# Turned-form products of a decoder block in fp32: joining two 256-column matmuls into one of 512

## The reference, cut to what matters

```python
def hybrid_layer(x, ...):
    h = rmsnorm(x, g_mix) @ w_in                       # [256, 2048] @ [2048, 5728]
    ...                                                # Mamba-2 scan and sparse attention
    x = x + jnp.concatenate([y_ssd, y_att], axis=-1) @ w_out
    u = rmsnorm(x, g_mlp) @ w_up                       # [2048, 8192]
    return x + jnp.square(jax.nn.relu(u)) @ w_down     # [8192, 2048]

def second_block(x, ...):
    h = fox_attention(rmsnorm_2(x, g0), w_in, b_f, w_out)   # q, k, v: 3 x [2048, 2048], 16 heads
    x = x + rmsnorm_2(h, g1)
    h = sqrelu_mlp(rmsnorm_2(x, g2), w1, w2)                # [2048, 8192], [8192, 2048]
    return x + rmsnorm_2(h, g3)
```

## Time and profile before

| | |
|---|---|
| median of 3 runs | 2294.41 us (2293.33 to 2296.01) |
| profiled execution, own time | 2293.16 us |
| its span | 2291.4 us |
| TensorE busy (matmul) | 2261.6 us, 99% |
| DVE busy | 1208.5 us, 53% |
| ACT busy | 946.4 us, 41% |
| DMA moved | 412.12 MB, mean 180 GB/s |
| granted TensorE clock, mean | 0.998 |

### The profile page before, as it was taken

The page is one execution under the profiler, slowest core; times in us unless marked ns, Lnnn a source line. Parts: engine busy times, 40 slices in busy tenths (PEclk is TensorE's granted clock), DMA queues, the critical chain, the costliest instruction groups (busy, mean ns, idle before and its releaser), DMA issues.

```text
span 2291.4 us, 32313 instructions
## 1 busy us (share of the span) xinstructions
PE 2261.6 (99%) x14211; PEld 2024.1 (88%) x14211; DVE 1208.5 (53%) x1167; ACT 946.4 (41%) x901; POOL 12.4 (1%) x34
## 2 busy tenths in 40 slices
PE   7999999999999999999999999999999999999998
PEld 7988778999988899988899987888998888999886
DVE  5688665545444354544455444555555443545444
ACT  5453564444433343434334434434435333434332
POOL 1000000000000000000000000000000000000000
PEclk9999999999999999999999999999999999999999
DMA  8445435666555666555555454555665556665554
GB/s 259 152 157 166 156 129 190 196 184 183 184 190 193 186 184 183 184 184 184 185 184 183 148 165 155 176 186 171 184 184 192 185 184 188 185 184 189 190 184 147
DMA packets 210908, 412.12 MB, mean 180 GB/s; under 512 B 12804, under 2 KB 12896, under 8 KB 210160
## 3 DMA queue, kind: packets, MB, share of 16 engines
q1 hardware_dynamic: 210368, 409.89, 55.7%
q0 software_dynamic: 432, 0.62, 0.2%
HBM read 408.39 MB, written 2.10 MB: 179 GB/s over the span
## 4 chain that ended last, share of the span: by engine, by line
PE 98%; DVE 1%; ACT 1%; DMA 0%; issue 0%; DVEq 0%; SPq 0%; ACTq 0%
PE bank L1705 16%; PE bank L1706 16%; PE bank L1707 16%; PE bank L1720 15%; PE bank L1723 15%; PE bank L1722 15%; PE bank L1803 1%; PE bank L1735 1%; PE bank L1828 0%; PE bank L1837 0%; PE bank L1922 0%; PE bank L1896 0%; PE bank L1815 0%; PE bank L1807 0%; PE bank L1829 0%; DMA G<-in_g_mix_dram 0%
## 5 line engine op out<-in xcount | busy, mean ns | idle before, releaser
L942 DVE TENSOR_TENSOR wl<-raw,wh 128x2048 fp32r<-128x2048 f32 x380 | 870.3, 2291 | 647.3 <-ACT wh L501 645.2
L501 ACT ACTIVATE wh<-raw 128x2048 fp32r<-128x2048 f32 x380 | 726.7, 1913 | 724.8 <-DMA raw<-in_mlp_w_dram 265.0
L1720 PE MATMUL bank<-XH,wh 128*128 128x256 f32 x2880 | 817.7, 284 | 0.2 <-issue 0.2
L1723 PE MATMUL bank<-XH,wl 128*128 128x256 f32 x2880 | 812.7, 282 | 0.0
L1722 PE MATMUL bank<-XL,wh 128*128 128x256 f32 x2880 | 810.3, 281 | 0.0
L1722 PEld LDWEIGHTS bank<-XL,wh 128*128 128x128 f32 x2880 | 547.2, 190 | 0.6 <-issue 0.5
L1720 PEld LDWEIGHTS bank<-XH,wh 128*128 128x128 f32 x2880 | 543.7, 189 | 3.7 <-issue 2.2
L1723 PEld LDWEIGHTS bank<-XH,wl 128*128 128x128 f32 x2880 | 542.8, 188 | 0.0
L1707 PE MATMUL bank<-wh,hl 128*128 128x512 f32 x1024 | 404.5, 395 | 0.0
L1706 PE MATMUL bank<-wl,hh 128*128 128x512 f32 x1024 | 404.4, 395 | 0.0
L1705 PE MATMUL bank<-wh,hh 128*128 128x512 f32 x1024 | 402.2, 393 | 0.0
(11 more groups left out here) (310 smaller groups left out, 819.7 us busy)
## 6 DMA issues: line engine op xcount, KB each, us to landing
raw<-in_mlp_w_dram SPq DMA_DIRECT2D x128, 1024.0 KB, 5.4
raw<-in_w_up_dram SPq DMA_DIRECT2D x64, 1024.0 KB, 5.5
raw<-in_w_down_dram SPq DMA_DIRECT2D x64, 1024.0 KB, 5.0
raw<-in_fox_w_in_dram SPq DMA_DIRECT2D x48, 1024.0 KB, 5.1
raw<-in_w_in_dram SPq DMA_DIRECT2D x44, 1024.0 KB, 5.0
raw<-in_w_out_dram SPq DMA_DIRECT2D x16, 1024.0 KB, 5.1
raw<-in_fox_w_out_dram SPq DMA_DIRECT2D x16, 1024.0 KB, 5.1
G<-in_norm_g_dram SPq DMA_DIRECT2D x4, 1024.0 KB, 5.9
```

The lines of the kernel that those rows point to most:

```text
L501: act.activation(wh[:, j, :, :], raw[:, j, :, :], ACT.Copy).then_inc(hi_ready, 1)
L942: dve.tensor_tensor(wl[:, j, :, :], raw[:, j, :, :], wh[:, j, :, :].bitcast(F32), ALU.subtract)\
L1720: pe.matmul(o, sh, mh, start=first and kk == 0 and f % 2 == 0, stop=False, skip_group_check=True)
L1723: mm = pe.matmul(o, sl, mh, start=False, stop=last and kk == 3, skip_group_check=True)
```

## The change

`XH` and `XL` become two halves of one tensor `XHL`, laid side by side for each k tile. A new form `half_cols` takes a panel as two half panels of 256 columns. For each k tile and 128-column block it issues one matmul of the high weights with 512 moving columns (high x, then low x) into a whole bank, and one of the low weights with high x into the left half of the same bank. The result of a block is then the sum of the bank's two halves. A half panel uses one pair of banks, so the numbering of accumulators changes (`up_acc`, `fox_acc`). The weights of a half panel come as two chunks of 8 k tiles by 256 columns (`half_panels`), still 1 MB each.

All turned panels of the MLPs and of the fox stage but the first of each use it; `WIN` does not. In the MLPs ACT copies the right half of each bank to `LP` (`part`), DVE adds it to the left half into `RB` and makes Relu and square in one instruction, and `high` and `low` follow on 256 columns. In the fox stage ACT copies the right half straight to `FQ` or `FK`, and DVE adds the left half and multiplies by the factor (`fox_part`), at every second slot, behind the attention work of that slot. The scores wait for a new semaphore, `fqk_ready`. The Fori loops of the MLPs are written out. The diff leaves out the old `relu`, `high`, `square`, `low` and `hidden`, which stand above, and a layout change of the instructions that write `XH` and `XL`.

```diff
-        XH = sb("XH", [P, KT, TOK], F32R)
-        XL = sb("XL", [P, KT, TOK], F32R)
+        XHL = sb("XHL", [P, KT, 2, TOK], F32R)
+        XH, XL = XHL[:, :, 0, :], XHL[:, :, 1, :]
...
+        def up_acc(half, n):
+            return 2 * n - (1 if half == 0 and n else 0)
+        O_DOWN = [up_acc(half, UP) for half in range(2)]
+        O_HALF = O_DOWN[0] + DOWN
+        B_FOX, O_FOX = B_M1 + 2 * B_HALF, O_M1 + O_HALF + O_DOWN[1] + DOWN
+        def fox_acc(n):
+            return O_FOX + (2 * n - (1 if n else 0) if n <= 8 else 7 + n)
...
+            def half_panels(w, b, col):
+                for j in range(4):
+                    sp.wait_ge(chunk_used, 4 * b + j - 3)
+                    c, r = col + 256 * (j // 2), 8 * P * (j % 2)
+                    sp.dma_start(raw[:, j, :, :].rearrange("p a (c n) -> p (a c) n", n=256),
+                                 w[r:r + 8 * P, c:c + 256].rearrange("(k p) n -> p k n", p=P))\
+                      .then_inc(raw_landed[j], 16)
...
-                    with sp.Fori(0, UP // 2 - 1) as i:
-                        for s in (1, 2):
-                            for j in range(4):
-                                chunk(w_a, b + 2 * i + s, j, 4 * j,
-                                      bass.ds(half * HALF + 512 * (2 * i + s), 512))
-                    panel(w_a, b + UP - 1, 0, half * HALF + 512 * (UP - 1))
+                    for n in range(1, UP):
+                        half_panels(w_a, b + n, half * HALF + 512 * n)
...
+                def whole(u, o, b):
+                    act.wait_ge(chunk_used, 4 * b + 4)
+                    for k in range(2):
+                        act.wait_ge(hl_ready, 2 * u + k + 1)
+                        act.activation(RB[:, k, :], acc[o % 2][k][:, :], ACT.Relu).then_inc(acc_freed[o % 2][k], 1)
+                def part(u, o, b, j):
+                    act.wait_ge(chunk_used, 4 * b + j + 1)
+                    for k in range(2):
+                        act.wait_ge(sq_ready, 2 * u)
+                        act.activation(LP[:, k, :], acc[o % 2][k][:, TOK:], ACT.Copy).then_inc(part_ready, 1)
+                def high(u, tile, wide):
+                    for k in range(2):
+                        act.wait_ge(sq_ready, 2 * u + k + 1)
+                        f = 2 if wide else 1
+                        act.activation(hh[:, tile + f * k:tile + f * k + f, :],
+                                       RB[:, k, 0:f * TOK].rearrange("p (f t) -> p f t", f=f), ACT.Copy)\
+                           .then_inc(hh_ready, 1)
+                def hidden(j, half, n, b):
+                    if j >= 2:
+                        if half == 0 and n == 0:
+                            return
+                        u, e, wide, tile = up_acc(half, n), 1, False, 4 * n
+                    else:
+                        n, b = n - 1, b - 1
+                        if n < 0:
+                            return
+                        u, e, wide, tile = up_acc(half, n + 1) - 1, 3, half == 0 and n == 0, 4 * n + 2
+                        if wide:
+                            tile = 4 * n
+                    o, u = o0 + half * O_HALF + u, u0 + half * U_HALF[0] + u
+                    if j % 2:
+                        high(u, tile, wide)
+                    elif wide:
+                        whole(u, o, b)
+                    else:
+                        part(u, o, b, e)
...
+            def fox_part(n, j):
+                acc_o = fox_acc(n) + j // 2
+                act.wait_ge(chunk_used, 4 * (B_FOX + n) + j + 1)
+                kind, f = FOX[n][0], 4 * (n // 2) + j - 1
+                for k in range(2):
+                    dst = FQ if kind == "fq" else FK
+                    act.activation(dst[:, f + k, :], acc[acc_o % 2][k][:, TOK:], ACT.Copy)\
+                       .then_inc(step["fqk_part"], 1)
...
             def fox_side(n):
+                if 1 <= n // 4 <= 8 and n % 4 in (0, 2):
+                    p, e = n // 4 - (n % 4 == 0), 3 if n % 4 == 0 else 1
+                    if 1 <= p <= 7:
+                        fox_part(p, e)
                 if n == 3:
                     root(2, 2)
...
+                def square(u, o, wide):
+                    for k in range(2):
+                        if wide:
+                            dve.wait_ge(acc_freed[o % 2][k], o // 2 + 1)
+                            dve.tensor_tensor(RB[:, k, :], RB[:, k, :], RB[:, k, :], ALU.mult).then_inc(sq_ready, 1)
+                        else:
+                            dve.wait_ge(hl_ready, 2 * u + k + 1)
+                            dve.wait_ge(part_ready, 2 * (u - u // U_HALF[1] - (1 if u % U_HALF[1] else 0)) + k + 1)
+                            dve.tensor_tensor(RB[:, k, 0:TOK], acc[o % 2][k][:, 0:TOK], LP[:, k, :], ALU.add)\
+                               .then_inc(acc_freed[o % 2][k], 1)
+                    if not wide:
+                        for k in range(2):
+                            dve.wait_ge(acc_freed[o % 2][k], o // 2 + 1)
+                            dve.scalar_tensor_tensor(out=RB[:, k, 0:TOK], in0=RB[:, k, 0:TOK], scalar=0.0,
+                                                     in1=RB[:, k, 0:TOK], op0=ALU.max, op1=ALU.mult)\
+                               .then_inc(sq_ready, 1)
+                def low(u, tile, wide):
+                    f = 2 if wide else 1
+                    for k in range(2):
+                        dve.wait_ge(hh_ready, 2 * u + k + 1)
+                        at = slice(tile + f * k, tile + f * k + f)
+                        dve.tensor_tensor(hl[:, at, :], RB[:, k, 0:f * TOK].rearrange("p (f t) -> p f t", f=f),
+                                          hh[:, at, :].bitcast(F32), ALU.subtract).then_inc(hl_ready, 1)
+                def hidden(j, half, n):
+                    if j >= 2:
+                        if half == 0 and n == 0:
+                            return
+                        u, wide, tile = up_acc(half, n), False, 4 * n
+                    else:
+                        n = n - 1
+                        if n < 0:
+                            return
+                        u, wide = up_acc(half, n + 1) - 1, half == 0 and n == 0
+                        tile = 4 * n if wide else 4 * n + 2
+                    o, u = o0 + half * O_HALF + u, u0 + half * U_HALF[0] + u
+                    if j % 2:
+                        low(u, tile, wide)
+                    else:
+                        square(u, o, wide)
...
+            def fox_part(n, j):
+                acc_o = fox_acc(n) + j // 2
+                kind, f = FOX[n][0], 4 * (n // 2) + j - 1
+                dst = FQ if kind == "fq" else FK
+                for k in range(2):
+                    dve.wait_ge(step["fqk_part"], 4 * n - 4 + j - 1 + k + 1)
+                    dve.tensor_tensor(dst[:, f + k, :], acc[acc_o % 2][k][:, 0:TOK], dst[:, f + k, :], ALU.add)\
+                       .then_inc(acc_freed[acc_o % 2][k], 1)
+                for k in range(2):
+                    dve.wait_ge(acc_freed[acc_o % 2][k], acc_o // 2 + 1)
+                dve.scalar_tensor_tensor(out=dst[:, f:f + 2, :], in0=dst[:, f:f + 2, :],
+                                         scalar=SCALE if kind == "fq" else 1.0,
+                                         in1=RCf[:, :].unsqueeze(1).broadcast_to([P, 2, TOK]),
+                                         op0=ALU.mult, op1=ALU.mult).then_inc(step["fqk_ready"], 1)
...
                     attn_probs(1, (n - 18) // 2, Lf, FST)
+                if 1 <= n // 4 <= 8 and n % 4 in (0, 2):
+                    p, e = n // 4 - (n % 4 == 0), 3 if n % 4 == 0 else 1
+                    if 1 <= p <= 7:
+                        fox_part(p, e)
...
-                    if j == 0 and prev:
+                    if j == 0 and prev and not 2 <= n <= 8:
                         take(*prev)
-                prev = (kind, O_FOX + n, seen.get(kind, 0), B_FOX + n)
+                prev = (kind, fox_acc(n), seen.get(kind, 0), B_FOX + n)
...
+            def half_cols(b, o):
+                for j in range(4):
+                    x, e = o + j // 2, j % 2
+                    if e == 0:
+                        acc_wait(x)
+                    pe.wait_ge(lo_ready, 4 * b + j + 1)
+                    for kk in range(8):
+                        k = 8 * e + kk
+                        at = 256 * (kk % 2)
+                        for f in range(2):
+                            bk = acc[x % 2][f]
+                            sh, sl = (z[:, j, kk // 2, at + f * P:at + (f + 1) * P] for z in (wh, wl))
+                            pe.matmul(bk[:, :].rearrange("p (s t) -> p s t", s=2), sh, XHL[:, k, :, :],
+                                      start=k == 0, stop=False, skip_group_check=True)
+                            mm = pe.matmul(bk[:, 0:TOK], sl, XH[:, k, :], start=False, stop=k == KT - 1,
+                                           skip_group_check=True)
+                    mm.then_inc(chunk_used, 1)
+                    yield j
```

(76 more changed lines are left out.)

94 lines of the change are left out of this document (41 added, 53 removed).

## The result

The changed kernel takes 2281.29 us (median of 4 runs, 2279.7 to 2281.62) where the kernel before took 2295.21 us (2293.33 to 2296.66): ratio 0.994, 95% interval 0.9928 to 0.9952, 13.9 us less. The forecast was 2280.5 us and 13.9 us less.

What follows compares the result with a forecast made beforehand. TensorE at 2.4 GHz, 98% of the chain, was taken as the bound. Joining saves 13.9 us; ACT, DVE and DMA add nothing: 2294.4 - 13.9 = 2280.5 us, range 2268 to 2295.

Steps and rivals of the forecast that it cites:

- The price of a pair: TensorE, `half_cols`: a 512-column and a 256-column matmul take 232.0 + 119.0 = 351.0 ns, against 356.9 for three of 256.
- the sum: TensorE, MLPs and fox stage: 37 changed panels of 64 pairs, 5.9 ns saved on each of 2368 pairs, 13.9 us.
- a sign of being wrong: TensorE, up panels: a 256-column matmul behind a 512-column one costing other than 119 ns would show the forecast wrong.
- The chain: ACT and DVE, MLP up panels: last product to next chunk's weights ready takes 5.04 us, wanted after 5.62, no wait.
- Rival (a): TensorE pairs: both weight loads hide, 348 ns a pair, 21 us saved, 2273.4 us; chance 0.12.
- Rival (b): TensorE pairs: only the fixed part per instruction is saved, 2.5 ns a pair, 5.9 us, 2288.5 us; chance 0.06.
- Rival (c): TensorE pairs: joining does nothing, the mixed order costs 356.9 ns, 2294 us; chance 0.05.
- Rival (d): MLP up half panels: ACT's two waiting points bound; at 6.1 us, 60 stalls of 0.48 us, net 15 slower, 2309; chance 0.13.
- The fox order: Fox stage: DVE's emptying behind the attention step costs nothing; probabilities ready at 11.99 us, turn due at 12.88, slack 0.9.
- The 97 ns of the prediction: DMA queues, kernel before: time of each hardware packet, 3.1 us for an engine's 32 packets of a chunk.
- The bound of 64 ns for 1 KB: DMA queues, half-panel weights: a 1 KB packet costs at most 64 ns, 4.1 us a chunk, hidden under 5.62.

## Why the prediction was right

**The price of a pair.** 351.0 ns forecast, 351.7 measured, and undoing the joining alone takes back the gain: that kernel is 0.5 us from the kernel before, inside the interval. That each stream is priced by start to start, and not by its duration, is what made the sum: 0.6% of the time hangs on 5 ns in 357. The split within the pair was less exact than its sum. The prediction had 232 and 119 ns; the traces show 234.0 and 117.7, two errors of opposite sign. It named a narrow matmul that costs other than 119 as a sign of being wrong, and by 1.3 ns that sign appeared. It carries little, since the runs with other widths show that the records can put time behind the wrong one of a pair. But the price of a mixed order was assumed from two pure ones, and that the errors cancel to 0.7 ns is in part luck: the other orders of the same matmuls cost 1.7 ns less.

**Where it sits.** In the MLPs a half panel fell from 11.42 to 11.253 us, 0.17 rather than the 0.19 of the sum: 60 x 0.17 = 10 us. In the fox stage two slots fell from 13.17 to 12.90 us on average, 0.27; from the stage's first high part to that of the next stage it is 310.4 against 306.7 us, 3.7 us less, where the sum had 2.7; with the joining undone it is 310.4 again. The two small errors cancel in the total. Why a pair saves more in the fox stage is open.

**The bounds of the pair.** Rival (a), 348 ns, is not reached in any order; 350.0 is the least seen with all the work. Rival (b), 2.5 ns a pair, is out by the pair itself, which fell by 5.2 ns (356.9 to 351.7), and by the total, 13.9 us and not 5.9. The formula of the Trainium skill in "TensorE: Matmul & The Clock Gate", section "Back-to-back issue gap", would also give 384 columns 162.5 ns, and they went at 175. Rival (c) is out by the run that undoes the joining.

**ACT and DVE cost nothing.** The chain was forecast at 5.04 us and came to 5.05; its slack holds one extra copy and not three. Rival (d) was priced rightly in kind, and about 0.1 us too low for each half panel: past the slack TensorE pays the lateness and 0.1 us on top. What kept it away is 0.58 us.

**The fox order.** Behind the attention step it costs nothing, as forecast, with 1.09 us left before the turn (1262.58 less 1261.49) where 0.9 was forecast. Ahead of it, it costs more than twice the whole gain of the change.

**The transfers.** The 97 ns of the prediction is the mean over all packets, narrow ones included; the packet records of that trace give 102 ns for those of 2 KB. The bound of 64 ns for 1 KB was safe and loose: 53 ns, so 3.4 us a chunk against 3.3 before, and landing stayed at 5.5 us. That a packet of 1 KB would not cost as much as one of 2 KB was what the narrow weights' landing told, and the runs of 512 B confirm it.

## What to carry to other kernels

On a TensorE that is never idle, price a change of form by start-to-start distances taken over whole panels of the trace; durations gave no price here. Before emptying is moved, follow the one chain from "last product" to "next chunk's weights ready" in the order of each engine's list, and compare it with a chunk's time: here the slack was 0.58 us, and a chain 1.35 us longer turned 14 us won into 36 us lost. A wait for TensorE's boundary belongs behind whatever TensorE itself wants at that boundary.

## What the runs showed of the hardware that was not expected

- Eight TensorE waits of 2.8 us cost 36 us, over half as much again as they last. Seven of them were followed by a stretch with a low granted clock (0.50 from 1251 to 1257 us, matmuls 0.43 us apart instead of 0.23), one was not, and that one cost 3.1 us in all.
- A start of TensorE that is 0.77 or 0.37 us late at the upper clock level cost about 0.1 us more than its lateness (12.12 and 9.82 us a half panel): the matmul behind the wait held the next one off for 0.34 us instead of 0.23.
- The order of wide and narrow matmuls matters a little: 351.7 ns a pair in turn, whether in two banks or in one, and 350.0 ns by twos and by fours. Why, no run here tells, and in the fox stage the gain is absent.
- At the upper clock level fp32r streams cost 117.7 to 119 ns for 256 columns, 175 for 384 and 232 to 234 for 512, 0.453 to 0.465 ns a column, some 9% to 12% over one column a cycle of 2.4 GHz. What takes them stays open.
- A stream of 128 columns next to one of 512 costs 106 to 108 ns, hardly less than the 117.7 of one of 256, and the records show the loss behind the wide matmul, not behind the narrow one.
